# A two-layer trunk: keys turned once and loaded per step in the delta scan, the tables' order, and the scale of x by logarithm

## The reference

```
h    = rmsnorm(x, norm_w[l])                 # x * rsqrt(mean(x*x) + 1e-6) * w
proj = h @ w_in[l]                           # delta q,k,v (4 heads of 128), z, b, a; attention q,k,v,z
q, k, v of the delta branch: convolution over 5 tokens and silu; q and k then l2-normed
y_dn = gated delta rule over the sequence, forward and backward, both summed
       beta = sigmoid(b); g = -exp(a_log) * softplus(a + dt_bias)
       S_t = exp(g_t) S_(t-1) (I - beta_t k_t k_t^T) + beta_t k_t v_t^T;  o_t = S_t^T q_t
       then rmsnorm of o and silu(z)
y_at = grouped attention, 8 heads on 2 key heads of 64, with rotary positions, gated by silu(z)
x    = x + concat(y_dn, y_at) @ w_out[l]
```

## Time and profile before

| | us |
|---|---|
| median of three runs (4128.55 to 4132.61) | 4130.52 |
| the profiled execution | 4140.22 |
| its span | 4138.4 |
| layer 0: projection, from 4.30 | 663.6 |
| layer 0: tables, from 667.85 | 27.25 |
| layer 0: delta opening, from 695.10 | 90.7 |
| layer 0: scan and its end, from 785.8 | 327 |
| layer 0: attention and output projection, from 1113 | 944.5 |
| layer 1: projection, from 2057.5 | 642.3 |
| finish, from 4093.7 | 44 |

### The profile page before, as it was taken

One profiled execution on the slowest core, in us unless ns is written; L12 is line 12 of the kernel. 1 busy time (PEld: TensorE's weight loads), 2 busy tenths in 40 slices (PEclk: granted clock), 3 DMA queues, 4 the chain that ended last, 5 costly groups with the idle time before them and its releaser, 6 DMA issues. The chain is left out here.

```text
span 4138.4 us, 55812 instructions
## 1 busy us (share of the span) xinstructions
PE 3777.8 (91%) x19078; PEld 2942.7 (71%) x19078; DVE 2813.9 (68%) x3424; ACT 1872.0 (45%) x2552; POOL 716.5 (17%) x761
## 2 busy tenths in 40 slices
PE   7999996698799999999999999965997999999896
PEld 5877785488667776767778777845985776677674
DVE  5674183566699999975266723735677999999733
ACT  4222212255377777772122222132554777777511
POOL 0022101596400000000001211036952000000000
PEclk8999997899899999999999999977998999999997
DMA  2112174545520000005321113654454200000335
GB/s 112 73 67 77 64 245 138 135 135 150 157 113 25 22 25 24 22 22 175 151 97 72 62 72 130 219 141 124 137 163 142 73 22 24 25 22 21 97 139 228
DMA packets 335765, 407.71 MB, mean 99 GB/s; under 512 B 105872, under 2 KB 255504, under 8 KB 315224
## 3 DMA queue, kind: packets, MB, share of 16 engines
q1 hardware_dynamic: 332728, 384.67, 29.1%
q10 hardware_dynamic: 2880, 20.97, 1.2%
HBM read 265.70 MB, written 139.66 MB: 98 GB/s over the span
## 5 line engine op out<-in xcount | busy, mean ns | idle before, releaser
L1864 DVE TENSOR_REDUCE att_sb_part<-att_banks 128x1 f32<-128x512 f32 x992 | 679.9, 686 | 103.2 <-PE att_banks L1749 89.1
L1851 ACT ACTIVATE att_sb_probs<-att_banks 128x1024 f32<-128x1024 f32 x512 | 525.0, 1025 | 314.3 <-PE att_banks L1777 314.1
L1882 DVE TENSOR_TENSOR att_sb_p_lo<-att_sb_probs,att_sb_p_hi 128x1024 fp32r<-128x1024 f32 x512 | 622.5, 1216 | 20.6 <-ACT att_sb_p_hi L1855 20.6
L1855 ACT ACTIVATE att_sb_p_hi<-att_sb_probs 128x1024 fp32r<-128x1024 f32 x512 | 544.0, 1063 | 16.1
L341 PE MATMUL proj_banks<-proj_sb_h_hi,proj_sb_w_hi 128*128 128x512 f32 x1600 | 500.7, 394 | 9.8 <-DVE proj_sb_pad L535 9.8
L341 PE MATMUL proj_banks<-proj_sb_h_lo,proj_sb_w_hi 128*128 128x512 f32 x1600 | 498.7, 393 | 0.0
L341 PE MATMUL proj_banks<-proj_sb_h_hi,proj_sb_w_low 128*128 128x512 f32 x1600 | 498.0, 392 | 0.0
L401 POOL TENSOR_TENSOR c_low_squares<-c_sq_acc,proj_sb_high_squares 128x2048 fp32r<-128x2048 f32 x28 | 141.1, 5039 | 1680.2 <-ACT c_sq_acc L462 1680.2
L1777 PE MATMUL att_banks<-att_sb_q,att_sb_k 68*128 68x512 f32 x1024 | 409.7, 400 | 0.0
L1776 PE MATMUL att_banks<-att_sb_q,att_sb_k 128*128 128x512 f32 x1024 | 407.4, 398 | 1.9 <-DVE att_sb_q L1876 1.9
L1794 PE MATMUL att_banks<-att_sb_p_hi,att_sb_v_hi 128*65 128x512 f32 x1024 | 403.1, 394 | 1.4 <-DVE att_sb_p_lo L1882 1.4
(11 more groups left out here) (236 smaller groups left out, 5496.8 us busy)
## 6 DMA issues: line engine op xcount, KB each, us to landing
proj<-proj_sb_out SPq DMA_DIRECT2D x40, 1024.0 KB, 3.8
dn_sb_kq<-proj SPq DMA_DIRECT2D x64, 512.0 KB, 4.8
proj_sb_w_raw<-in_w_in SPq DMA_DIRECT2D x52, 536.0 KB, 3.6
dn_sb_room<-proj SPq DMA_DIRECT2D x32, 768.0 KB, 4.9
att_sb_q<-att_q SPq DMA_DIRECT2D x64, 256.0 KB, 2.6
x_res<-ahead_delta SPq DMA_DIRECT2D x16, 1024.0 KB, 4.1
proj_sb_pad<-proj SPq DMA_DIRECT2D x24, 512.0 KB, 4.7
proj<-proj_sb_out ACTq DMA_DIRECT2D x12, 1024.0 KB, 4.4
```

The lines of the kernel that those rows point to most:

```text
L1851: nc.scalar.activation(probs[:, pair % 2], ps[:, 2 * (pair % 2):2 * (pair % 2) + 2, :], ACT.Exp, scale=SCALE).then_inc(s["exp_done"], 1)
L1855: nc.scalar.activation(p_hi[:, pair % SLOTS], probs[:, pair % 2], ACT.Copy).then_inc(s["hi_done"], 1)
L1864: nc.vector.tensor_reduce(part[:, w // NQ, w % NQ:w % NQ + 1], ps[:, 4 + w % 2, :], AX.X, ALU.max) \
L1882: nc.vector.tensor_tensor(p_lo[:, pair % SLOTS], probs[:, pair % 2], p_hi[:, pair % SLOTS].bitcast(F32), ALU.subtract).then_inc(s["lo_done ...
```

## The change

The start stage goes: SP loads ones and ident last of layer 0's first loads, DVE sets eps in layer 0's projection. The scale of x comes from four products of ones with c.sq_acc (128x512 each), then on ACT Ln (with eps and 1/1024) of each and Exp of -0.5 times it; the 16 small products, Sqrt, reciprocal, diagonals, spreading products and copies go, in both projections and in `finish`. In layer 1 PE does tiles 0 to 2 before the first beta products, and ACT its part after round_h(2). In `finish` the last tile is multiplied and stored in two halves.

In the tables each load has its own semaphore, SP's order is ba, decay, sums, all masks (384 KB instead of 128; the delta stage reads them too and loads none), v; Ln and Sqrt stand ahead of the copies of v on ACT, beta and the norms ahead of the logarithm's part on DVE, beta's transpose ahead of the sums on PE; SP waits for b_rows only after it has issued att_v.

In the delta stage there are four chunk tiles. PE turns the keys of chunk n-1 after `local(n)` (4 transposes), ACT copies them, SP stores them (256 KB, dn_keys). In the scan `turn_k` is gone; SP loads the keys of both sides (256 KB each) at the end of step j for step j+1, behind load_dd and after state_step(j); ACT scales them in place between `carried_output` and `new_values`. The first transposes of v wait for the copied keys two chunks before, load_kqv for the turned ones.

```diff
+                if first_layer:
+                    sp.dma_start(c.ones[:], a.ones).then_inc(s["consts_loaded"], 16)
+                    sp.dma_start(c.ident[:], a.ident).then_inc(s["consts_loaded"], 16)
...
+                        pe.wait_ge(s["consts_loaded"], 32)
+                    for n in range(NQ):
+                        nc.tensor.matmul(ps[:, NQ + n, :], c.ones[:], c.sq_acc[:, n * QB:(n + 1) * QB],
+                                         start=True, stop=True).then_inc(s["x_sums"], 1)
...
-                    first_tile(0)
-                    first_tile(1)
-                    spread_scale()
-                    first_tile(2)
+                    for k in range(3):
+                        first_tile(k)
                     pe.wait_ge(s["ba_split"], 2)
-                    pe.wait_ge(s["scale_copied"], NQ)
-                    beta_decay(0)
+                    pe.wait_ge(s["x_log"], NQ)
+                    for k in range(3):
+                        beta_decay(k)
                     for k in range(3, KT - 1):
-                        beta_decay(k - 2)
                         first_tile(k)
-                    for k in range(KT - 3, KT):
                         beta_decay(k)
+                    beta_decay(KT - 1)
                     first_tile(KT - 1, halves)
...
+                    if first_layer:
+                        act.wait_ge(s["eps_set"], 1)
+                    for n in range(NQ):
+                        act.wait_ge(s["x_sums"], n + 1)
+                        nc.scalar.activation(scale[:, n * QB:(n + 1) * QB], ps[:, NQ + n, :], ACT.Ln, bias=c.eps[:, 0:1],
+                                             scale=1.0 / D_MODEL).then_inc(s["x_log"], 1)
+                    act.wait_ge(s["x_log"], NQ)
+                    for n in range(NQ):
+                        nc.scalar.activation(scale[:, n * QB:(n + 1) * QB], scale[:, n * QB:(n + 1) * QB], ACT.Exp,
+                                             scale=-0.5).then_inc(s["scale_ready"], 1)
...
+                sp.dma_start(ba[:], a.ba).then_inc(s["ba_loaded"], 16)
+                sp.dma_start(decay[:], a.decay[l].partition_broadcast(P)).then_inc(s["decay_loaded"], 16)
+                sp.dma_start(square_sums[:], a.dn_sums).then_inc(s["sums_loaded"], 16)
+                sp.dma_start(c.masks[:], a.masks).then_inc(s["masks_in"], 16)
                 for kv in range(KV_HEADS):
                     sp.dma_start(v[kv * DH:(kv + 1) * DH], a.proj[T_AK + kv].rearrange("(r c) t -> r c t", c=PAIR_HEADS)[:, KV_HEADS:]) \
                         .then_inc(s["v_loaded"], 16)
                 sp.wait_ge(s["copied"], 1)
                 sp.dma_start(a.b_rows.rearrange("c i t -> (c i) t"), rows[:]).then_inc(s["stored"], 16)
-                sp.wait_ge(s["stored"], 16)
                 sp.wait_ge(s["v_copied"], NQ)
                 sp.dma_start(a.att_v.rearrange("p c k d -> p c (k d)"), vt[:]).then_inc(s["v_stored"], 16)
+                sp.wait_ge(s["stored"], 16)
                 sp.wait_ge(s["v_stored"], 16)
...
+                pe.wait_ge(s["dve_step"], 17)
+                nc.tensor.transpose(ps[:, 0, 0:P], c.tok[:, T_BETA].rearrange("p c i -> p (c i)"), c.ident[:]) \
+                    .then_inc(s["turned"], 1)
+                pe.wait_ge(s["dve_step"], 19)
                 pe.wait_ge(s["sums_copied"], 1)
+                pe.wait_ge(s["masks_in"], 16)
...
+                act.wait_ge(s["dve_step"], 6)
+                nc.scalar.activation(ln[:], u[:], ACT.Ln).then_inc(s["act_step"], 1)
+                act.wait_ge(s["dve_step"], 10)
+                nc.scalar.activation(c.v_scale[:], kk[:].rearrange("p h c -> p c h"), ACT.Sqrt).then_inc(s["act_step"], 1)
...
+                dve.wait_ge(s["act_step"], 4)
+                nc.vector.tensor_tensor(ln[:], ln[:], g[:], ALU.subtract).then_inc(s["g_copied"], 1)
...
+                dve.wait_ge(s["turned"], 1)
+                nc.vector.tensor_copy(rows[:], ps[:, 0, 0:P]).then_inc(s["copied"], 1)
...
+                def store_keys(n):
+                    sp.wait_ge(s["kt_copied"], n + 1)
+                    sp.dma_start(a.dn_keys[CHUNK_ORDER[n]], turned_keys[:, n % 2])                         .then_inc(s[f"kt_stored{n % 2}"], 16)
+
+                def load_keys(i):
+                    for side in SIDES:
+                        if i:
+                            sp.wait_ge(s[f"ds{side}"], i)
+                        else:
+                            for n in range(2):
+                                sp.wait_ge(s[f"kt_stored{n}"], 16 * NC // 2)
+                        sp.dma_start(kk[:, side], a.dn_keys[chunk_of(side, i)]).then_inc(s[f"kt_loaded{side}"], 16)
...
-                for n in range(3):
+                for n in range(KQV_TILES):
...
                 for n in range(NC):
                     store_blocks(n)
-                    if n + 3 < NC:
-                        load_kqv(n + 3)
+                    if n:
+                        store_keys(n - 1)
+                    if n + KQV_TILES < NC:
+                        load_kqv(n + KQV_TILES)
...
+                store_keys(NC - 1)
                 load_dt(1)
+                load_keys(0)
...
                     if j + 2 < NC:
                         load_dd(j + 2)
+                    if j + 1 < NC:
+                        load_keys(j + 1)
...
+                def turn_keys(n):
+                    pe.wait_ge(s["vv"], n + 1)
                     for h in HEADS:
-                        mm = nc.tensor.transpose(turned(side)[:, h, :], kq[:, i % 2, side, DN_HEADS + h, :], c.ident[:])
-                    mm.then_inc(s[f"kt{side}"], 1)
+                        mm = nc.tensor.transpose(bank(3 * (n % 2) + 2)[:, h, :], kqv[:, n % KQV_TILES, 2 * DN_HEADS + h, :],
+                                                 c.ident[:])
+                    mm.then_inc(s["kt_turned"], 1)
...
+                    pe.wait_ge(s[f"kq_loaded{j % 2}"], 32 * (j // 2 + 1))
                     each(chain(side), kq[:, j % 2, side, KEY], state[:, side]).then_inc(s[f"ks{side}"], 1)
 
                 def carried(side, j):
-                    pe.wait_ge(s[f"kk{side}"], j + 1)
+                    if j:
+                        pe.wait_ge(s[f"oa{side}"], j)
                     each(turned(side), kq[:, j % 2, side, QUERY], state[:, side]).then_inc(s[f"carry{side}"], 1)
...
                     local(n)
+                    if n:
+                        turn_keys(n - 1)
+                turn_keys(NC - 1)
...
                     for side in SIDES:
                         solve(side, j)
-                    for side in SIDES:
-                        if more:
-                            turn_k(side, j + 1)
...
+                def copy_keys(n):
+                    act.wait_ge(s["kt_turned"], n + 1)
+                    if n >= 2:
+                        act.wait_ge(s[f"kt_stored{n % 2}"], 16 * (n // 2))
+                    nc.scalar.copy(turned_keys[:, n % 2], bank(3 * (n % 2) + 2)).then_inc(s["kt_copied"], 1)
+
                 def keys(side, i):
-                    act.wait_ge(s[f"kt{side}"], i + 1)
-                    if i:
-                        act.wait_ge(s[f"ds{side}"], i)
+                    act.wait_ge(s[f"kt_loaded{side}"], 16 * (i + 1))
                     for h, item in zip(HEADS, heads(side)):
-                        op = nc.scalar.activation(kk[:, side, h, :], turned(side)[:, h, :], ACT.Copy,
+                        op = nc.scalar.activation(kk[:, side, h, :], kk[:, side, h, :], ACT.Copy,
                                                   scale=c.tok[:, T_END, chunk_of(side, i), item:item + 1])
...
                     for side in SIDES:
                         carried_output(side, j)
                     for side in SIDES:
+                        keys(side, j)
+                    for side in SIDES:
                         new_values(side, j)
-                    if j + 1 < NC:
-                        for side in SIDES:
-                            keys(side, j + 1)
...
+                def scaled(k, cols):
+                    nc.vector.scalar_tensor_tensor(out=x[:, k, cols], in0=x[:, k, cols], scalar=w[:, k:k + 1],
+                                                   in1=r[:, cols], op0=ALU.mult, op1=ALU.mult).then_inc(s["normed"], 1)
+
```

More of the change, by code:

```diff
@@ L284, in first_tile @@
                             mm.then_inc(s["proj_done"], 1)
-                def spread_scale():
-                    for n in range(NQ):
-                        pe.wait_ge(s["diagonal"], n + 1)
-                        nc.tensor.matmul(ps[:, NQ + n, :], c.ones[:], scale[:, n * QB:(n + 1) * QB],
-                                         start=True, stop=True).then_inc(s["spread"], 1)
                 def beta_decay(k):
@@ L422, in round_ba @@
                     nc.scalar.copy(ba_w[:, :, 0:W_BA], ba_raw[:]).then_inc(s["ba_hi"], 1)
-                def copy_scale():
-                    for n in range(NQ):
-                        act.wait_ge(s["spread"], n + 1)
```

(26 more changed lines are left out.)

181 lines of the change are left out of this document (57 added, 124 removed).

## The result

The median went from 4130.84 to 4101.57 us (four runs each), a ratio of 0.9928 with a 95% interval of 0.9913 to 0.9944: 29.7 us less, 23 to 36. The forecast was 4092.0 with 4078 to 4112, a gain of 38.5. The direction and the range held; the gain was 6 to 9 us short.

What follows compares the result with a forecast made beforehand. TensorE was busy 91% of the span, but six edited places had different limits (serial chains, latency, VectorE, GpSimd, transfers). Savings 3.5 + 4.7 + 4.1 + 13.4 + 6.0 + 5.8 + 1.0 = 38.5 from 4130.5 gave 4092.0, range 4078 to 4112.

Steps and rivals of the forecast that it cites:

- Constants and scale, layer 0: Start stage and layer 0's scale chain: 3.5 saved by moving the constant loads, 4.7 by the shorter chain.
- The rival with the clock staying high: Layer 0's scale: all four quarters take 0.89, saving 7.4 instead of 4.7; part of a faster rival given 18%.
- The drain behind a table load: ScalarE in the tables: the skill's 1.38 drain per load would make the sum about 31; forecast stayed with 1.28.
- Tables: Tables' stage, both layers: att_v's store waits only for the v copies; 6.7 saved per layer, 13.4.
- rival C: v is the tables' floor, 3 later, and finish and layer 1 give their lower bounds: 4098; chance 17%.
- Projection, layer 1: Opening of layer 1's projection: two TensorE gaps, 1.10 and 3.03, go; 4.1 saved, bounds 3 and 5.
- Delta opening: Opening of the delta stage, both layers: removed load waits save 3.0 per layer, between 1.0 and 4.6.
- rival B: Openings and tails give nothing as another wait takes over, VectorE nearly full in the opening: 26.7, 4103.8; chance 20%.
- First eight steps: Scan: removed key transposes save nothing while TensorE waits for GpSimd, its idle grows; step 8 gives 1.1.
- Tail: Scan's last eight steps: 0.44 saved in each of steps 9 to 14, 0.8 lost in the last.
- Rival A: Scan: late key loads; each us beyond 3.9 goes 1:1 into a step, 4162 at 7.4; chance 3%.
- Finish: Finish, bound by its transfers: shorter scale chain and halved last store save 1.0, between 0.3 and 2.

Runs made afterwards that it cites:

- e1: Kernel before with only the constants' edit and the scale of x by logarithm (both projections and finish): 4115.78 us, ratio 0.9968.
- e8: Changed kernel with SP issuing the small beta loads of groups 1 to 4 behind the load of lanes 0: 4090.69 us, ratio 0.9899 to the kernel before.
- e12: Changed kernel with only v loaded ahead of the sums and the masks in the tables' stage: 4096.90 us, ratio 0.9919 to the kernel before.
- e2: Kernel before with only the tables' order and the single load of the masks, which the delta stage reads there: 4118.83 us, ratio 0.9969.
- e3: Kernel before with only the delta stage's edits (keys turned in the opening, stored and loaded, four chunk tiles), own masks load kept: 4124.80 us, ratio 0.9989.
- e4: Changed kernel with the key loads issued behind the next step's load_kq instead of ahead of it: 4196.39 us, ratio 1.0166 to the kernel before.
- e6: Changed kernel with three chunk tiles instead of four: 4110.49 us, ratio 0.9950 to the kernel before.
- e7: Changed kernel with keys turned in the scan as before, no key stores or loads, four tiles kept: 4099.39 us, ratio 0.9920 to the kernel before.
- e10: e8 with v ahead of the sums and masks in the tables, and new values ahead of the keys in the last step: 4097.41 us, ratio 0.9920.
- e9: e7 and e8 together: changed kernel with keys turned in the scan and SP's small beta loads moved: 4083.33 us, ratio 0.9889 to the kernel before.
- e11: e9 with v also loaded ahead of the sums and the masks in the tables' stage: 4090.96 us, ratio 0.9903 to the kernel before.
- e5: The changed kernel run once more, unedited, for a second profile: 4099.99 us, ratio 0.9921 to the kernel before.

## Why the prediction was right or wrong

**Constants and scale, layer 0: the sum right, its two terms not.** The tables begin 8.65 and 8.08 earlier, of 8.2. But in the eleven profiles without the start stage TensorE's sums begin at 52.05 to 53.61, and at 54.91 to 55.32 in the other three: 2.4 on the mean, not 3.5. In the first profile the first projection load is issued 3.55 earlier and TensorE's first product starts 3.1 earlier (11.70, not 14.84); where the rest goes no run here shows. The chain from the first sum to the whole scale takes 9.62 instead of 15.35, 5.7 less, not 4.7. The two misses cancel, which is luck. The rival with the clock staying high came in three of the eleven (e1, e8, e12): at a granted clock of 1.00 the four products took 3.70 instead of 5.40, and the chain 8.42, 6.9 less, where I had said 7.4 (the numbers given there make 7.2).

**The drain behind a table load: the row was right.** Ln, load, Exp follow each other here without the 1.38 that the Trainium skill, "ScalarE: Activation LUTs", section "What ACT_TABLE_LOAD costs", puts behind a load. e2 gave 12.8 (9.1 to 16.5) for the tables, where that rule would have left 7.8.

**Tables: right**, 12.7 and 12.8 of 13.4. att_v's store is the end, v's landing the floor, and rival C's 3 us delay of v is not in the trace of layer 0 (v landed 0.9 later after its issue than before). Layer 1 comes nearer to it: v landed 2.3 later after its issue, 11.78 into the stage instead of 10.49, and the stage took 21.55.

**Projection, layer 1: the opening was right, the stage short by 0.8.** Timeline of the changed kernel, answering:

```profile
2047.22 2.05 PE L277 MATMUL proj_banks<-proj_sb_h_hi,proj_sb_w_hi 128*128 128x512 f32 x4 [3.01 <-ACT proj_sb_h_hi L394]
...
2056.82 1.08 PE L286 MATMUL proj_banks<-proj_sb_h_hi,proj_sb_ba_w 128*32 128x512 f32 x4
...
2057.16 2.19 ACT L411 ACTIVATE proj_sb_scale<-proj_sb_scale 128x512 f32<-128x512 f32 x4
```

TensorE goes from tile 2 into the beta products without a gap, and its first product behind the opening starts 49.86 into the stage instead of 54.16, 4.3 less. After that, windows of 100 us of the changed kernel and of the one before:

```profile
2087.68:2187.68 100.00, 100.00 (x427) 81.51 (x428) 66.72 (x41) 18.20 (x13) 0.00 (x0) 0.98 0.18 70
```

```profile
2111.65:2211.65 100.00, 100.00 (x434) 81.60 (x435) 68.20 (x42) 18.21 (x13) 0.00 (x0) 1.00 0.19 70
```

In the first the granted clock is 0.98 and 427 products run, in the second 1.00 and 434; the stretch to the stage's end is 589.64 instead of 588.15. The three profiles with the old opening (before, e2, e3) have 642.1 to 643.5 for the stage, the eleven with the new one 638.7 to 640.4, on the mean 3.3 less: about 1 of the 4.3 is given back, and in this pair the clock shows where.

**Delta opening: the size was near, the step failed.** I wrote that VectorE is the busiest engine there and the added transposes, copies and issues "lie beside" it, costed them at nothing, and took 3.0 per layer. The premise was wrong in the kernel before already. Windows of its opening and of the changed kernel's (us, then PE, PEld, DVE, ACT, POOL busy, PE's clock, DMA share, GB/s):

```profile
695.10:785.80 90.70, 69.06 (x390) 50.13 (x391) 52.74 (x95) 30.33 (x82) 38.65 (x26) 0.93 0.65 175
```

```profile
679.47:768.67 89.20, 76.56 (x448) 57.15 (x448) 51.97 (x95) 35.90 (x95) 38.90 (x26) 0.93 0.76 210
```

TensorE is busy 69.1 of 90.7 us, VectorE 52.7, so rival B's "nearly full" is wrong too. (The ends of matmuls are modelled in the profile, so this is no measure of how full TensorE is, but VectorE has far more room than I thought.) TensorE also stands 13.6 for chunk loads there, in six waits in layer 0, of which I had counted the first, 3.52; now these are 0.8. The added work fills part of that: TensorE's busy time grows by 7.5 and the time between two chunks from 3.94 to 4.37. The lengths of all profiles (us):

| opening | layers 0 / 1 |
|---|---|
| three tiles, keys in the scan, own masks (before; e1) | 90.71 / 92.17; 90.64 / 91.11 |
| the same, masks from the tables' stage (e2) | 89.48 / 89.32 |
| changed (two profiles; e4; e12) | 89.20 / 90.17, 87.94 / 86.65; 89.48 / 88.09; 90.05 / 86.95 |
| three tiles (e6) | 95.34 / 94.52 |
| keys in the scan (e7) | 85.05 / 87.44 |
| SP's order (e8; e10) | 86.34 / 86.53; 86.89 / 86.93 |
| both (e9; e11) | 80.02 / 79.66; 82.15 / 81.84 |

On the mean the changed opening has 88.6 and the old one 91.2: 2.6 per layer of the 3.0, and e2 has 1.8 of that from the masks alone. With SP's order of e8 the price of the added work shows: 86.7 with the keys in the opening (e8, e10), 80.9 without (e9, e11), 5.8 per layer. That is near 15 chunks at the 0.43 more that each takes on TensorE (4.37 in e8, 3.94 in e9). In the changed kernel's order only 2.3 of it shows (e7). So the term that I put at nothing is 2 to 6 per layer, and the size came out near only because what I gave for the removed waits was too small as well. That is luck again.

Before, for SP's load of lanes 0 and VectorE's preparation of them (timeline):

```profile
730.83 0.71 SPq L1008 DMA_DIRECT2D dn_sb_lane_raw<-w_blk  x1
...
737.17 1.21 DVE L1487 TENSOR_TENSOR dn_sb_lane_mat<-dn_sb_lane_raw,dn_sb_lane_beta 64x1024 f32<-64x1024 f32 x1
```

and the changed kernel, whose delta stage begins 15.63 earlier:

```profile
717.91 0.86 SPq L989 DMA_DIRECT2D dn_sb_lane_raw<-w_blk  x1
...
723.68 1.22 DVE L1487 TENSOR_TENSOR dn_sb_lane_mat<-dn_sb_lane_raw,dn_sb_lane_beta 64x1024 f32<-64x1024 f32 x1 [4.89 <-DMA dn_sb_lane_raw<-w_blk]
...
768.67 0.25 POOL L1397 TENSOR_TENSOR dn_sb_lane_tmp<-dn_sb_lane_mat,dn_sb_lane_inv 128x31 f32<-128x31 f32 x1 [19.10 <-DVE dn_sb_lane_mat L1489]
```

Lanes 0 were issued 35.7 us into the stage, now 38.4 (in layer 1 37.7 and 36.4): TensorE no longer waits for loads, but SP does not finish its list sooner. It issues four chunk loads (6.48; three took 4.68), the norm weights and beta's loads without a pause to 700, then four stores, a key store and a load per chunk. VectorE waits 4.89 for lanes 0, where it had waited for nothing; in exchange its wait of 3.50 for the next lanes shrinks to 0.72. In layer 0 e8, which moves the list, issues lanes 0 at 34.0, e7, which takes the key stores and the transposes out, at 35.9, and e9, which does both, at 29.7; VectorE begins on them at 40.25, 41.40 and 36.00, where the changed kernel has 44.21. GpSimd's idle before its run fell from 21.89 to 19.10. The fourth tile is worth more than I said: 12 us in all with the keys turned in the opening (e6), and about 3 per layer without (e7's openings against e2's). With three tiles e6's TensorE waits 11.8 us for loads in that opening, no more than the 13.6 of before, and its added work comes on top; that turning the keys keeps a tile longer adds to it is not shown.

**First eight steps: right that the removed transposes give nothing**, wrong that the idle would grow in step 8. Step 8 and what follows in the changed kernel, answering:

```profile
962.17 3.78 PE L1149 MATMUL dn_banks<-dn_sb_room 128*128 128x128 f32 x16 [7.60 <-DVE dn_sb_room L1503]
965.75 3.06 PE L1149 MATMUL dn_banks<-c_sq_acc,dn_sb_room 128*128 128x128 f32 x16
```

TensorE's wait there is 7.60, and two others of these steps are longer. From the list of TensorE's waits of the changed kernel (us, times, longest):

```profile
PE dn_banks L1149 <- DMA c_sq_acc<-d_blk: 29.3, 4, 18.1
PE dn_banks L1199 <- DVE dn_sb_room L1522: 11.1, 1, 11.1
```

Before, the same two were 22.5 and 8.5. All of TensorE's waits from GpSimd's start to step 9 add up to 53.6, against 52.6 before, so the idle hardly grew at all. Windows of that stretch, before and changed:

```profile
785.81:991.50 205.69, 155.77 (x1438) 149.39 (x1435) 116.97 (x206) 88.28 (x297) 175.85 (x275) 0.88 0.42 118
```

```profile
768.67:973.91 205.24, 153.76 (x1361) 147.96 (x1360) 115.15 (x206) 91.74 (x296) 175.39 (x275) 0.84 0.51 146
```

TensorE runs 77 instructions fewer and is busy only 2.0 us less, at a granted clock of 0.84 instead of 0.88: what the transposes leave free the rest takes up at the lower level. And the 1.1 for step 8 didn't come: from this solve to the next known start it is 11.75 before and 11.74 now. Windows of the changed kernel there:

```profile
962.17:968.60 6.43, 6.43 (x32) 6.43 (x33) 2.86 (x7) 4.67 (x17) 0.00 (x0) 0.54 0.22 57
968.60:973.90 5.30, 5.30 (x66) 4.96 (x65) 3.91 (x7) 0.57 (x2) 3.33 (x3) 1.00 0.46 142
```

The granted clock is 0.54 (the lower level, 1.2 GHz, nearly throughout) for the 6.4 us behind the stall and 1.00 after. Before, it was 0.57 from 979.75 to 984.40, when solve and the transposes ran, and 1.00 after. Without the transposes the 16 products that follow run in the slow stretch, 3.06 instead of 1.95.

**Tail: right in kind, size 0.38 instead of 0.44 per step.** From the start of step 9 (973.91) to that of step 15 (1068.00) are six steps of 15.68 on the mean, against 16.06. The loads, the wait and the last step:

```profile
996.42 2.45 ACT L1313 ACTIVATE dn_sb_room<-dn_sb_room,c_tok 128x128 f32<-128x128 f32 x8 [0.93 <-DMA dn_sb_room<-dn_keys]
...
997.66 0.66 PE L1230 MATMUL dn_banks<-c_ident,dn_sb_room 128*128 128x128 f32 x4 [0.15 <-POOL dn_sb_room L1422]
...
1077.33 3.95 PE L1149 MATMUL dn_banks<-dn_sb_room 128*128 128x128 f32 x32 [0.63 <-ACT dn_sb_room L1336]
```

ScalarE waited 0.74 to 0.93 for keys in three of the seven tail steps of layer 0, within the microsecond counted; in the second profile (e5) one such wait, in step 9, is 1.33, over the 1 us that I had named as a sign of being wrong, and that step took 16.28. TensorE's second half waits 0.15 for the normalized values; the last step lost 0.76 where I had said 0.8. Rival A did not happen, but e4 shows that its mechanism is real and that my price per us was too low, since it left the clock out.

**Finish: right**, 0.96 and 0.89 of 1.0. The scale was ready 4.2 earlier, the transfers stayed full, answering:

```profile
4075.00:4091.00 16.00, 0.00 (x0) 0.00 (x0) 5.49 (x4) 0.00 (x0) 0.00 (x0) 0.50 1.00 424
```

**The sum.** Against the timed parts: e1 holds the terms 3.5 + 4.7 + 4.1 + 1.0 = 13.3 and measured 13.2, e2 the 13.4 and measured 12.8, e3 the 6.0 + 5.8 = 11.8 and measured 4.5. By these medians the delta stage is 7.3 of the missing 8.0, but how it splits is open. e3's interval is 0.8 to 8, and e3 keeps its own load of the masks, whose part of the opening's 6.0 is in e2. Single profiles show 8.8 (e3), 9.3 and 14.5 for the delta stage, so a profiled stage scatters by nearly as much as the miss. Over all profiles the opening gives 2.6 per layer and the scan behind it 2.2 (325.2 with loaded keys, 327.4 with keys turned in the scan), 9.5 in all of 11.8. With 0.7 of the tables and 0.8 of the projection that makes about 4 of the 6 to 9 us missing; the rest no profile shows. The profile before was slow in the untouched stage, so subtracting from the median was right.

## What to carry to other kernels

When a wait on a load is removed, look at the queue that issues the next load as an engine of its own: count its issues up to the one that decides, and the added ones among them. A small transfer put behind a large one landed with or behind the large one in both places where it was tried here; order a queue by when each thing is wanted and keep the small early ones ahead. Before an engine is called the busiest of a stage, read its busy time and all of its waits in that stage's window. Work moved out of a full loop into an opening costs there what it takes, unless every engine and queue of the opening has room for it.

## What the runs showed of the hardware

One issue on SP took 0.45 us in the median of the changed kernel's 1539, and 0.3 to 0.7 in nine of ten, but the load of the norm weights, one column over 128 partitions, held SP for 3.11 us (685.99 in the changed kernel). A 256 KB load landed 3.0 us after its issue with nothing large ahead and 5.2 behind 1 MB. The load of the sums was waited for until 7.3 after its issue behind v (e12), where the changed kernel used it 4.1 after its issue without a wait. Removing 8 transposes right behind a stall of TensorE in step 8 gave nothing (11.75 and 11.74 to the next step), as the 16 products that follow took their place at a granted clock of 0.54 (3.06 instead of 1.95). The four products for the scale of layer 0 ran at a granted clock of 1.00 in three profiles of eleven (3.70 us) and partly at 0.50 in the other eight (5.40).
